# Seven block products in place of eight for the gate and up tiles of a dense feed-forward

## The chip, the cores and the metric
The kernel runs on one core of a Trainium2 chip. Its time is device microseconds (us) of one execution. The engines are TensorE (PE), VectorE (DVE), ScalarE (ACT), GpSimd (POOL) and SyncE (SP), which issues most of the DMAs.

## What is computed
A backbone of two layers over 512 tokens (256 of context, 256 latent) of width 1024. Each layer is a norm, a mixed token stage, a norm and a feed-forward; layer 0 has a dense one, layer 1 experts. The change is in the dense one:

```python
def swiglu(t, w_gu, w_down):
    g, u = jnp.split(t @ w_gu, 2, axis=-1)
    return (jax.nn.silu(g) * u) @ w_down
# layer 0: t is 512 x 1024 float32, w_gu 1024 x 5632, w_down 2816 x 1024
```

## The kernel before
Tokens lie along the free axis: the state is held transposed, as eight 128-row tiles of 512 columns (columns 0 to 255 are context, 256 to 511 latent). Every float32 product is made from three float32r ones: each operand is split in a high part (a rounded copy, made on ACT) and a low part (the operand less its high part, on DVE), and `three` issues high x high, high x low and low x high as three matmuls into one PSUM tile. The state is split once per norm into `hhi` and `hlo`. The weights stream through `raw`, five slots filled by SP's DMAs, and are split unit by unit into `whi` and `wlo`, three slots each (`split_hi` L623, `split_lo` L628), three units ahead of TensorE.

The feed-forward runs in two blocks of 11 column tiles (`FJ`). In a block, each tile j has a gate unit and an up unit of 1024 columns (8 k-tiles of 128x128). `fm_tile` makes each with 8 x 3 matmuls of 512 columns. ACT takes silu of the gate from PSUM into `sg`, DVE multiplies it with the up tile into `hf` (L2155), ACT rounds that into `fhi` (L1573), POOL makes `flo` (L1708). Then eight down units of 1408 columns (11 k-tiles) follow; each gives 33 matmuls of 512 columns and DVE adds the result to `xT` (L2162). Two gate/up tiles share the first walk over k (`two_tiles`), since the state comes tile by tile from the norm.

Order between engines is by semaphores, and each engine runs its own list in order: `split_used` counts units that TensorE is done with, `hi_ready` and `lo_ready` the splits, `sg_ready`, `fh_ready`, `fhi_ready`, `flo_ready` the steps after a pair, `down_out` the down tiles. SP loads a unit when the unit five before it has its low part.

The modulation of layer 1 is made in between: its weights land in `nraw` and `lraw`, TensorE multiplies them at the norms, ACT copies a row to `modrow`, `mod_turns` transposes it on TensorE (L744), and `mods_in` reduces it on DVE. `TURN_AT` says after which unit of the block `mod_turns` is called; the next call waits for `mod_out` of the last. In this kernel:

```python
TURN_AT = {6: NORM1[1] // 2 + 1, 8: NORM1[3] // 2 + 1}
```

## Time and profile before

| | us |
|---|---|
| time, median of 3 runs (1382.73 to 1383.71) | 1383.51 |
| the profiled execution | 1380.24 |
| its span, first to last instruction | 1378.4 |
| first gate/up stretch and second, about 364 to 487 and 549 to 672 | 123 each |
| the down tiles behind each | 62 and 62 |
| mean granted TensorE clock, as a share of full speed | 0.974 |

The page gives busy time and its share of the span for each engine, then the span in 40 slices of 34.5 us in tenths. A timeline row is start, duration, engine, line, operation, output and inputs with their sizes; in brackets the engine's idle time before it and what ended it. "x2" is two instructions in one row, its duration from the first's start to the last's end. Matmuls overlap, so the distance between their starts counts, not their duration.

### The profile page before, as it was taken

To read this page: it belongs to the slowest core of one execution; us is meant where nothing else is said; L and a number is where in the kernel's file an instruction comes from. 1 tells how busy PE (TensorE), PEld (TensorE's weight loads), DVE (VectorE), ACT (ScalarE), POOL (GpSimd) and SP (SyncE) were. 2 spreads that over 40 slices of the span, in tenths; PEclk is the share of its full clock that TensorE was granted. 3 is DMA by queue.
4 is the path that set the end of the run, shared out by engine and by line. 5 is a ranking of instruction groups with operands and counts; after the bars stand their busy time and mean duration, and the time that the engine had idled before them with its cause. 6 is when DMAs were issued, how large, how long until landed. Compare 5 with 4: busy or idle time off the path is not lost.

```text
span 1378.4 us, 19621 instructions
## 1 busy us (share of the span) xinstructions
PE 1284.8 (93%) x7072; PEld 1010.4 (73%) x7072; DVE 812.1 (59%) x1185; ACT 685.9 (50%) x977; POOL 115.8 (8%) x86
## 2 busy tenths in 40 slices
PE   4999977799999999999999987788999999999997
PEld 1688744458688888888886984476888888888876
DVE  2222686753533332332335657666988988988896
ACT  5422342552622221322325543355877877887784
POOL 2200000002011100111120000011000000000070
PEclk9999979899999999999999998899999999999999
DMA  9532246247222322223311354637999999999995
GB/s 357 152 107 92 77 157 242 92 154 271 64 93 94 127 84 77 92 92 117 113 58 53 123 166 179 235 125 284 401 353 375 389 360 363 402 365 359 389 383 208
DMA packets 96847, 283.30 MB, mean 206 GB/s; under 512 B 8704, under 2 KB 10256, under 8 KB 96528
## 3 DMA queue, kind: packets, MB, share of 16 engines
q1 hardware_dynamic: 90880, 264.27, 53.5%
q0 software_dynamic: 3600, 12.58, 2.5%
q10 hardware_dynamic: 2304, 5.58, 1.0%
q8 instruction: 43, 0.70, 0.2%
q14 instruction: 20, 0.16, 0.0%
HBM read 270.86 MB, written 11.53 MB: 205 GB/s over the span
## 4 chain that ended last, share of the span: by engine, by line
PE 81%; DVE 8%; ACT 5%; DMA 3%; issue 2%; SPq 0%; ACTq 0%; DVEq 0%
PE ps L751 13%; PE ps L753 13%; PE ps L752 13%; PE ps L1193 6%; PE ps L1195 6%; PE ps L1194 6%; PE ps L1210 3%; PE ps L1212 3%; PE ps L1208 3%; PE ps L728 2%; DMA raw<-in_w_mod 2%; PE ps L844 2%; PE ps L845 2%; PE ps L846 2%; DVE wlo L628 1%
## 5 line engine op out<-in xcount | busy, mean ns | idle before, releaser
L628 DVE TENSOR_TENSOR wlo<-raw,whi 128x1024 fp32r<-128x1024 f32 (+2 forms) x271 | 350.8, 1310 | 251.3 <-ACT whi L623 249.7
L623 ACT ACTIVATE whi<-raw 128x1024 fp32r<-128x1024 f32 (+2 forms) x271 | 298.1, 1107 | 208.6 <-PE ps L753 138.1
L751 PE MATMUL ps<-hhi,whi 128*128 128x512 f32 (+1 forms) x736 | 275.7, 375 | 7.6 <-DVE hlo L1845 5.9
L752 PE MATMUL ps<-hlo,whi 128*128 128x512 f32 (+1 forms) x736 | 272.8, 371 | 0.0
L753 PE MATMUL ps<-hhi,wlo 128*128 128x512 f32 (+1 forms) x736 | 272.7, 371 | 0.0
L751 PEld LDWEIGHTS ps<-hhi,whi 128*128 128x128 f32 x736 | 138.7, 188 | 41.8 <-issue 10.6
L753 PEld LDWEIGHTS ps<-hhi,wlo 128*128 128x128 f32 x736 | 138.7, 188 | 26.8
L752 PEld LDWEIGHTS ps<-hlo,whi 128*128 128x128 f32 x736 | 138.9, 189 | 25.9
L628 DVE TENSOR_TENSOR xlo<-raw,xhi 128x1024 fp32r<-128x1024 f32 (+1 forms) x98 | 134.4, 1374 | 29.1 <-ACT xhi L623 28.2
L623 ACT ACTIVATE xhi<-raw 128x1024 fp32r<-128x1024 f32 (+1 forms) x98 | 114.3, 1167 | 37.6 <-PE ps L1212 19.6
L1193 PE MATMUL ps<-whi,hs_hi 128*128 128x512 f32 (+1 forms) x256 | 95.4, 373 | 0.9 <-DVE hs_lo L2221 0.9
L1195 PE MATMUL ps<-whi,hs_lo 128*128 128x512 f32 (+1 forms) x256 | 93.2, 364 | 0.0
L1194 PE MATMUL ps<-wlo,hs_hi 128*128 128x512 f32 (+1 forms) x256 | 93.2, 364 | 0.0
L753 PE MATMUL ps<-fhi,wlo 128*128 128x512 f32 x176 | 69.3, 394 | 0.0
L752 PE MATMUL ps<-flo,whi 128*128 128x512 f32 x176 | 69.3, 394 | 0.0
L751 PE MATMUL ps<-fhi,whi 128*128 128x512 f32 x176 | 69.3, 394 | 0.0
L1573 ACT ACTIVATE fhi<-hf 128x512 fp32r<-128x512 f32 x22 | 13.9, 632 | 99.2 <-DVE hf L2155 99.2
L728 PE MATMUL ps<-raw,c_act 128*2 128x512 f32 x272 | 42.8, 706 | 18.1 <-DMA raw<-in_w_mod 17.3
L1700 POOL TENSOR_TENSOR rs<-rs,sq 128x512 f32<-128x512 f32 (+1 forms) x24 | 39.8, 1656 | 223.7 <-ACT sq L1325 223.0
L2162 DVE SCALAR_TENSOR_TENSOR xT<-ps,mod,xT 128x256 f32<-128x256 f32 x32 | 14.0, 479 | 74.1 <-PE ps L753 74.1
L1193 PEld LDWEIGHTS ps<-whi,hs_hi 128*128 128x128 f32 x256 | 48.1, 188 | 9.3 <-issue 1.9
L1195 PEld LDWEIGHTS ps<-whi,hs_lo 128*128 128x128 f32 x256 | 48.1, 188 | 8.2
(336 smaller groups left out, 2056.0 us busy)
## 6 DMA issues: line engine op xcount, KB each, us to landing
raw<-in_w_gu SPq DMA_DIRECT2D x230, 512.0 KB, 5.9
raw<-in_w_dn SPq DMA_DIRECT2D x80, 704.0 KB, 8.4
raw<-in_w_mod SPq DMA_DIRECT2D x68, 512.0 KB, 4.5
raw<-in_w_fm SPq DMA_DIRECT2D x32, 512.0 KB, 3.5
raw<-in_w_out SPq DMA_DIRECT2D x16, 512.0 KB, 4.2
y_rows<-zrow POOLq DMA_DIRECT2D x1, 5120.0 KB, 20.7
mraw<-in_w_mod SPq DMA_DIRECT2D x8, 512.0 KB, 5.9
raw<-in_w_tg SPq DMA_DIRECT2D x8, 512.0 KB, 3.5
```

Source lines behind the costliest of these rows:

```text
L623: nc.scalar.activation(high(v)[:, 0:cols], src[:, 0:cols], ACT.Copy).then_inc(hi_ready, 1)
L628: nc.vector.tensor_tensor(low(v)[:, 0:cols], landed_in(v)[0][:, 0:cols], high(v)[:, 0:cols].bitcast(F32), ALU.subtract).then_inc(lo_ready, 1)
L728: mm = nc.tensor.matmul(ps[32 * kk:32 * kk + 2, PAIR_BANK(n), :], c_act[:, 4 * half + kk, :], units[kk // 2][0][:, kk % 2 * 512:kk % 2 * 5 ...
L751: nc.tensor.matmul(outp, whs, xh, start=first, stop=False)
L752: nc.tensor.matmul(outp, whs, xl, start=False, stop=False)
L753: return nc.tensor.matmul(outp, wls, xh, start=False, stop=last)
L1193: nc.tensor.matmul(o, hs_hi[:, k, :], wh, start=(k == 0), stop=False)
L1194: nc.tensor.matmul(o, hs_hi[:, k, :], wl, start=False, stop=False)
L1195: mm = nc.tensor.matmul(o, hs_lo[:, k, :], wh, start=False, stop=(k == KT - 1))
L1208: nc.tensor.matmul(o, ehi[:, j, :], high(v)[:, w:w + n], start=(j == 0), stop=False, skip_group_check=True)
L1210: nc.tensor.matmul(o, ehi[:, j, :], low(v)[:, w:w + n], start=False, stop=False, skip_group_check=True)
L1212: mm = nc.tensor.matmul(o, elo[:, j, :], high(v)[:, w:w + n], start=False, stop=(j == FJ - 1), skip_group_check=True)
```

## The change
The 512 tokens are halved (context, latent), the eight k-tiles are halved, and gate and up are the two halves of the output: a 2 x 2 x 2 block product. A scheme with seven products of blocks makes it in place of eight. `part_product` makes one product: 4 k-tiles x 3 matmuls of 256 columns. Four of the seven use sums and differences of weight blocks (`weight_sum`, four 128x512 operations on POOL for each pair, into `sq` and `xn`), four use sums of state blocks (made once, on DVE, in `h_sums`, `h_differences` and `t_lo`). Each part of the weights, 512 columns, is split by itself, eight parts ahead (`part_hi_of`, `part_lo_of`), into eight windows of the old `whi` and `wlo`. DVE combines the products from PSUM (`combine`, five operations) into the gate in `sg` and the up tile in `hf`; ACT takes silu of `sg`, DVE multiplies the two (`up_gated`).

The first three pairs of block 0 are made as before, and under them the state's sums: `h_sums` before unit 0's step on DVE, `h_differences` in unit 1's, the low parts in the steps of units 2, 3 and 5. The other 8 pairs of block 0 and all 11 of block 1 are groups of seven. The modulation's last transposes move from units 6 and 8 to 1 and 2, because `mr4` takes the place of `modrow`; the four units in `lraw` are loaded after block 1's gate/up tiles, because `tm` lies there. Many semaphores of two layers become one that counts on; what waits for what stays. The core of the diff (renamed semaphores and their waits are left out):

```diff
--- before.py
+++ after.py
...
-        modrow = sb("modrow", [P, 2, 512])
+        part = ExitStack()
+        modrow = sb("modrow", [P, 2, 512], F32, part)
+        part.close()
+        mr4 = sb("mr4", [P, 4, CTX], F32R)
...
+        fsum = sb("fsum", [P, 2, FJ, T], F32, part)
...
+        tm = sb("tm", [P, 19, CTX], F32R, region)
...
+        def wide(x, a):
+            return fsum[:, x, a:a + 2, :].rearrange("p a (b n) -> p (a b) n", n=CTX)
+
+        x12, x22, t3 = wide(1, 9), wide(1, 7), wide(1, 5)
+        t1, t2, t4 = wide(0, 9), wide(0, 7), wide(0, 5)
...
+        J0, JN, G0 = (3, 0), (FJ - 3, FJ), (0, FJ - 3)
+        PARTS = 7
+        S2, S1, S3, S4 = sq[:, 0, :], sq[:, 1, :], xn[:, 0, :], xn[:, 1, :]
+        S_OF = {1: (S2, 2), 3: (S3, 3), 4: (S1, 1), 6: (S4, 4)}
...
-        TURN_AT = {6: NORM1[1] // 2 + 1, 8: NORM1[3] // 2 + 1}
+        TURN_AT = {1: NORM1[1] // 2 + 1, 2: NORM1[3] // 2 + 1}
...
+        def place7(i, p):
+            return (p + 6 + min(max(p // PARTS - 2, 0), 4 if i else 1)) % 8
...
+        def part_hi_of(act, i, p):
+            n, x = p // PARTS, p % PARTS
+            kind, q = before_part(i, p)
+            if kind == "part":
+                counted(act, part_done, split_used, i, q)
+            else:
+                act.wait_ge(split_used, i * BLOCK + V0 + q + 1)
+            if x in S_OF:
+                act.wait_ge(wsum_ready, 4 * (G0[i] + n) + S_OF[x][1])
+            else:
+                unit_landed(act, i, unit_of(i, n, x == 5))
+            q = place7(i, p)
+            count_one(nc.scalar.activation(whf[:, 512 * q:512 * q + 512], part_source(i, p), ACT.Copy),
+                      part_hi, hi_ready, p)
+
+        def part_lo_of(dve, i, p):
+            counted(dve, part_hi, hi_ready, i, p)
+            q = place7(i, p)
+            count_one(nc.vector.tensor_tensor(wlf[:, 512 * q:512 * q + 512], part_source(i, p),
+                                              whf[:, 512 * q:512 * q + 512].bitcast(F32), ALU.subtract),
+                      part_lo, lo_ready, p)
...
+                sp.wait_ge(split_used, (blocks - 1) * BLOCK + v0 + 2 * FJ)
+                for unit in norm2u:
+                    dst, arrived, _count = mod_landed(unit[1], unit[2])
+                    sp.dma_start(dst, source(unit)[0]).then_inc(arrived, 16)
...
+            def part_product(i, p):
+                n, x = p // PARTS, p % PARTS
+                g = G0[i] + n
+                counted(pe, part_lo, lo_ready, i, p)
+                if g == 0:
+                    if x == 0:
+                        pe.wait_ge(sg_ready[0], J0[0])
+                    if x == 1:
+                        pe.wait_ge(fh_ready[0], J0[0])
+                    if x in (1, 3, 4, 5):
+                        pe.wait_ge(tlo_ready, {1: 1, 3: 2, 4: 5, 5: 4}[x])
+                elif x == 0:
+                    pe.wait_ge(first_out, g)
+                elif x in (1, 3, 4, 6):
+                    pe.wait_ge(comb_out, 5 * (g - 1) + {1: 1, 3: 2, 4: 4, 6: 5}[x])
+                if i and n == 0 and x == 3:
+                    pe.wait_ge(down_out[0], i * KT + 1)
+                xh, xl = [(lambda k: hhi[:, k, 0:CTX], lambda k: hlo[:, k, 0:CTX]),
...
+                bank = (0, 2, 1, 5, 4, 3, 6)[x]
+                for k in range(4):
+                    c = 512 * place7(i, p) + P * k
+                    mm = three(ps[:, bank, 0:CTX], whf[:, c:c + P], wlf[:, c:c + P], xh(k), xl(k),
+                               k == 0, k == 3)
+                count_one(mm, part_done, split_used, p)
...
+                            if r in TURN_AT:
+                                mod_turns(TURN_AT[r])
+                    for p in range(PARTS * JN[i]):
+                        part_product(i, p)
+                    pe.wait_ge(comb_out, 5 * (G0[i] + JN[i] - 1) + 4)
...
+            def gate_silu(l, i, n):
+                act.wait_ge(comb_out, 5 * (G0[i] + n) + 5)
+                j = J0[i] + n
+                nc.scalar.activation(sg[:, j % 2, :], sg[:, j % 2, :], ACT.Silu).then_inc(sg_ready[l], 1)
...
+                        if r == 2:
+                            t_hi(tm[:, 0:4, :], t2, t_ready, 2)
+                            t_hi(tm[:, 8:12, :], t3, hsum_ready, 3)
+                        if r == 3:
+                            act.wait_ge(modT_done, NORM1[3] // 2 + 1)
+                            t_hi(mr4[:, :, :], t4, t_ready, 3)
+                        if r == 2 * J0[i] - 1:
+                            act.wait_ge(split_used, v0 + 2 * J0[i])
+                            t_hi(hhi[:, B12[0], B12[1]], t1, t_ready, 1)
...
+                    for n in range(JN[i]):
+                        g, j = G0[i] + n, J0[i] + n
+                        for x in range(PARTS):
+                            if x == 0:
+                                if i * FJ + j >= 2:
+                                    act.wait_ge(flo_ready[l], i * FJ + (j - 1))
+                                counted(act, part_done, split_used, i, PARTS * n)
+                                nc.scalar.activation(hf[:, j % 2, 0:CTX], ps[:, 0, 0:CTX], ACT.Copy
+                                                     ).then_inc(first_out, 1)
+                            if PARTS * n + x + 8 < PARTS * JN[i]:
+                                part_hi_of(act, i, PARTS * n + x + 8)
+                            if x == 1 and n:
+                                up_hi(l, i, j - 1)
+                            if x == 6:
+                                gate_silu(l, i, n)
+                            for r in range(2 * FJ, 2 * FJ + H):
+                                if behind_part(i, r) == PARTS * n + x:
+                                    unit_landed(act, i, v0 + r)
+                                    counted(act, part_done, split_used, i, PARTS * n + x)
+                                    nc.scalar.activation(high(v0 + r), landed_in(v0 + r)[0], ACT.Copy
+                                                         ).then_inc(hi_ready, 1)
...
+            def weight_sum(i, n, m):
+                g = G0[i] + n
+                a1, a2 = (landed_in(unit_of(i, n, up))[0] for up in range(2))
+                out, in0, in1, op, x = [(S1, a2[:, 0:512], a2[:, 512:1024], ALU.add, 4),
+                                        (S2, S1, a1[:, 0:512], ALU.subtract, 1),
+                                        (S3, a1[:, 0:512], a2[:, 0:512], ALU.subtract, 3),
+                                        (S4, a1[:, 512:1024], S2, ALU.subtract, 6)][m]
+                if m < 2:
+                    unit_landed(pool, i, unit_of(i, n, 1 - m))
+                if g:
+                    counted(pool, part_lo, lo_ready, *((i, PARTS * (n - 1) + x) if n else (0, PARTS * (JN[0] - 1) + x)))
+                if m in (1, 3):
+                    pool.wait_ge(wsum_ready, 4 * g + m // 2 + 1)
+                nc.gpsimd.tensor_tensor(out, in0, in1, op).then_inc(wsum_ready, 1)
...
+                pool.wait_ge(hlo_done, 2 * KT)
+                up_lo(l, 0, 0)
+                for m in range(4):
+                    weight_sum(0, 0, m)
+                for j in range(1, J0[0]):
+                    up_lo(l, 0, j)
...
+                    for n in range(JN[i]):
+                        if n + 1 < JN[i]:
+                            for m in range(4):
+                                weight_sum(i, n + 1, m)
+                        elif i + 1 < blocks:
+                            pass
+                        if n:
+                            up_lo(l, i, J0[i] + n - 1)
+                    up_lo(l, i, FJ - 1)
+                    if i + 1 < blocks:
+                        for m in range(4):
+                            weight_sum(i + 1, 0, m)
...
+            def h_sums():
+                dve.wait_ge(mod_used, NORM1[-1] + 1)
+                dve.wait_ge(hlo_done, 2 * KT)
+                for out, (ks, cs) in ((x12, B12), (x22, B22)):
+                    V.tensor_tensor(out, hhi[:, ks, cs].bitcast(F32), hlo[:, ks, cs].bitcast(F32), ALU.add
+                                    ).then_inc(hsum_ready, 1)
+                dve.wait_ge(hsum_ready, 1)
+                then(V.tensor_tensor(t1, x12, h1, ALU.subtract))
+                V.tensor_tensor(t1, t1, l1, ALU.subtract).then_inc(t_ready, 1)
+
+            def h_differences():
+                dve.wait_ge(t_ready, 1)
+                V.tensor_tensor(t2, x22, t1, ALU.subtract).then_inc(t_ready, 1)
+                dve.wait_ge(hsum_ready, 2)
+                V.tensor_tensor(t3, x22, x12, ALU.subtract).then_inc(hsum_ready, 1)
+                dve.wait_ge(t_ready, 2)
+                then(V.tensor_tensor(t4, h2, t2, ALU.subtract))
+                V.tensor_tensor(t4, t4, l2, ALU.add).then_inc(t_ready, 1)
+
+            def up_gated(l, i, j):
+                dve.wait_ge(sg_ready[l], i * FJ + (j + 1))
+                dve.wait_ge(comb_out, 5 * (G0[i] + j - J0[i]) + 4)
+                V.tensor_tensor(hf[:, j % 2, :], hf[:, j % 2, :], sg[:, j % 2, :], ALU.mult).then_inc(fh_ready[l], 1)
+
...
+            def combine(l, i, n, x):
+                g, j = G0[i] + n, J0[i] + n
+                p1, u3, u2 = hf[:, j % 2, 0:CTX], hf[:, j % 2, CTX:T], sg[:, j % 2, CTX:T]
+                if x >= 2:
+                    counted(dve, part_done, split_used, i, PARTS * n + x)
+                if x == 2:
+                    dve.wait_ge(first_out, g + 1)
+                    V.tensor_tensor(sg[:, j % 2, :].rearrange("p (a n) -> p a n", a=2), ps[:, 1:3, 0:CTX],
+                                    p1.rearrange("p (a n) -> p a n", a=1).broadcast_to([P, 2, CTX]), ALU.add
+                                    ).then_inc(comb_out, 1)
+                if x == 3:
+                    dve.wait_ge(comb_out, 5 * g + 1)
+                    V.tensor_tensor(u3, ps[:, 5, 0:CTX], u2, ALU.add).then_inc(comb_out, 1)
+                if x == 4:
+                    dve.wait_ge(comb_out, 5 * g + 2)
+                    V.tensor_tensor(u2, ps[:, 4, 0:CTX], u2, ALU.add).then_inc(comb_out, 1)
+                if x == 5:
+                    dve.wait_ge(comb_out, 5 * g + 2)
+                    V.tensor_tensor(hf[:, j % 2, :].rearrange("p (a n) -> p a n", a=2), ps[:, 3:5, 0:CTX],
+                                    u3.rearrange("p (a n) -> p a n", a=1).broadcast_to([P, 2, CTX]), ALU.add
+                                    ).then_inc(comb_out, 1)
+                if x == 6:
+                    dve.wait_ge(comb_out, 5 * g + 3)
+                    V.tensor_tensor(u2, ps[:, 6, 0:CTX], u2, ALU.add).then_inc(comb_out, 1)
 
             def ffn(l, v0, blocks):
...
+                    if i == 0:
+                        h_sums()
...
+                        if r == 1:
+                            h_differences()
+                        if r - 1 in TURN_AT:
+                            mods_in(TURN_AT[r - 1])
+                        if r == 2:
+                            t_lo(tm[:, 4:8, :], t2, tm[:, 0:4, :], 1)
+                            t_lo(tm[:, 12:16, :], t3, tm[:, 8:12, :], 2)
+                        if r == 3:
+                            t_lo(tm[:, 16:18, :], t4[:, 0:2, :], mr4[:, 0:2, :], 3)
+                            t_lo(rs2[:, :, :], t4[:, 2:4, :], mr4[:, 2:4, :], 3)
+                        if r == 2 * J0[i] - 1:
+                            t_lo(hlo[:, B12[0], B12[1]], t1, hhi[:, B12[0], B12[1]], 4)
+                        for p in first_parts(r):
+                            part_lo_of(dve, i, p)
+                    if i == 0:
...
+                    for n in range(JN[i]):
+                        for x in range(PARTS):
+                            if x == 0 and n:
+                                up_gated(l, i, J0[i] + n - 1)
+                            combine(l, i, n, x)
+                            if PARTS * n + x + 8 < PARTS * JN[i]:
+                                part_lo_of(dve, i, PARTS * n + x + 8)
...
```

## Rows read from the trace of the kernel before

**Rows 1.** The page's busy time by engine, and POOL's 40 slices.
```profile
PE 1284.8 (93%) x7072; PEld 1010.4 (73%) x7072; DVE 812.1 (59%) x1185; ACT 685.9 (50%) x977; POOL 115.8 (8%) x86
POOL 2200000002011100111120000011000000000070
```

**Rows 2.** Windows over the gate/up stretches: PE, PEld, DVE, ACT, POOL, clock, DMA share, GB/s.
```profile
364.00:487.00 123.00, 123.00 (x531) 98.78 (x530) 41.32 (x44) 40.00 (x52) 14.23 (x11) 1.00 0.31 101
...
549.00:672.00 123.00, 123.00 (x528) 98.58 (x528) 37.84 (x33) 36.66 (x45) 14.19 (x11) 1.00 0.32 103
```

**Rows 3.** Timeline of PE, 512 columns in layer 0, then 256 in layer 1.
```profile
439.86 0.39 PE L751 MATMUL ps<-hhi,whi 128*128 128x512 f32 x1
...
444.06 0.39 PE L751 MATMUL ps<-hhi,whi 128*128 128x512 f32 x1
...
924.82 0.28 PE L751 MATMUL ps<-hhi,whi 128*128 128x256 f32 x1
...
928.90 0.28 PE L751 MATMUL ps<-hhi,whi 128*128 128x256 f32 x1
```

**Rows 4.** Timeline of one gate/up pair: POOL, DVE, ACT, DVE.
```profile
439.40 1.29 POOL L1708 TENSOR_TENSOR flo<-hf,fhi 128x512 fp32r<-128x512 f32 x1 [9.91 <-ACT fhi L1573]
440.30 1.46 DVE L628 TENSOR_TENSOR wlo<-raw,whi 128x1024 fp32r<-128x1024 f32 x1 [1.65 <-ACT whi L623]
443.56 0.60 ACT L1569 ACTIVATE sg<-ps 128x512 f32<-128x512 f32 x1 [3.29 <-PE ps L753]
445.14 1.22 DVE L628 TENSOR_TENSOR wlo<-raw,whi 128x1024 fp32r<-128x1024 f32 x1 [3.37 <-ACT whi L623]
```

**Rows 5.** Timeline at the output projection: DVE, then POOL.
```profile
318.57 1.23 DVE L628 TENSOR_TENSOR wlo<-raw,whi 128x1024 fp32r<-128x1024 f32 x1 [0.28 <-ACT whi L623]
319.14 1.81 POOL L1700 TENSOR_TENSOR rs<-rs,sq 128x512 f32<-128x512 f32 x1 [144.81 <-ACT sq L1325]
```

**Rows 6.** Timeline at the end of layer 1: POOL, then DVE.
```profile
1331.29 2.65 POOL L1737 TENSOR_TENSOR htm<-htm 128x1024 f32<-128x1024 f32 x1
1333.92 4.88 POOL L1734 TENSOR_SCALAR hf<-hf,gate 128x1024 f32<-128x1024 f32 x1
...
1331.60 0.41 DVE L2274 TENSOR_TENSOR eact<-esg,ps 128x256 f32<-128x256 f32 x1
1331.93 0.41 DVE L2229 TENSOR_TENSOR elo<-ps,ehi 128x256 fp32r<-128x256 f32 x1
1332.26 2.77 DVE L628 TENSOR_TENSOR wlo<-raw,whi 128x1024 fp32r<-128x1024 f32 x1
...
1332.26 3.90 DVE L628 TENSOR_TENSOR wlo<-raw,whi 128x1024 fp32r<-128x1024 f32 x2
```

**Rows 7.** Timeline of DVE in the norm, two operations back to back.
```profile
361.13 0.69 DVE L1833 TENSOR_TENSOR xn<-xT,rs 128x512 f32<-128x512 f32 x1
361.74 0.69 DVE L1845 TENSOR_TENSOR hlo<-sq,hhi 128x512 fp32r<-128x512 f32 x1
```

**Rows 8.** Timeline of ACT and DVE: the splits of the first down unit.
```profile
477.65 1.37 ACT L623 ACTIVATE whi<-raw 128x1408 fp32r<-128x1408 f32 x1
...
479.06 1.62 DVE L628 TENSOR_TENSOR wlo<-raw,whi 128x1408 fp32r<-128x1408 f32 x1 [3.21 <-ACT whi L623]
```

**Rows 9.** Timeline at the start of block 0 (DVE, ACT), and at tile 8.
```profile
367.10 0.69 DVE L1845 TENSOR_TENSOR hlo<-sq,hhi 128x512 fp32r<-128x512 f32 x1 [1.01 <-ACT hhi L1339]
...
375.91 0.60 ACT L1569 ACTIVATE sg<-ps 128x512 f32<-128x512 f32 x1 [1.28 <-PE ps L753]
...
407.65 0.18 DVE L1790 TENSOR_REDUCE modsum<-ps 128x8 f32<-128x32 f32 x1
...
409.32 0.60 PE L744 MATMUL ps<-ident,modrow 128*128 128x128 f32 x4
```

**Rows 10.** Windows in layer 0's attention stage (columns as in rows 2).
```profile
238.00:240.00 2.00, 0.00 (x0) 0.00 (x0) 1.93 (x5) 1.54 (x5) 0.00 (x0) 0.67 0.04 8
...
242.00:244.00 2.00, 1.88 (x8) 1.57 (x8) 1.90 (x6) 0.00 (x0) 0.00 (x0) 0.50 0.00 0
244.00:246.00 2.00, 1.86 (x5) 0.51 (x4) 1.93 (x7) 1.88 (x5) 0.00 (x0) 0.62 0.00 0
```

More of the change, by code:

```diff
@@ new lines, in meets, with before_part, behind_part @@
+        def meets(i, p, r):
+            a, b = unit_cols(r)
+            return 512 * place7(i, p) < b and a < 512 * place7(i, p) + 512
+        def before_part(i, p):
+            for q in range(p - 1, -1, -1):
+                if place7(i, q) == place7(i, p):
+                    return "part", q
+            units = (3, 4, 5) if i == 0 else (-3, -2, -1)
+            return "unit", max(r for r in units for q in range(p + 1) if meets(i, q, r))
+        def behind_part(i, r):
+            return max(p for p in range(PARTS * JN[i]) if meets(i, p, r)
+                       and not any(place7(i, q) == place7(i, p) for q in range(p + 1, PARTS * JN[i])))
@@ new lines, in part_lo_of, with first_parts @@
+        def part_lo_of(dve, i, p):
[4 more added lines that the diff above has]
+                      part_lo, lo_ready, p)
+        def first_parts(r):
+            i, r = (0, r) if r < 2 * J0[0] else (1, r - BLOCK)
+            return [p for p in range(8) if before_part(i, p) == ("unit", r)]
@@ L541, in _ @@
             sp.wait_ge(split_used, V_OUT[0] + 1)
-            for unit in norm1u + norm2u:
+            for unit in norm1u:
                 dst, arrived, _count = mod_landed(unit[1], unit[2])
@@ L1562, in ffn @@
                 for i in range(blocks):
-                    for r in range(BLOCK):
+                    for r in range(2 * J0[i]):
                         j = r // 2
-                        if r < 2 * FJ and r % 2 == 0:
-                            act.wait_ge(split_used, i * BLOCK + (v0 + r + 1))
+                        if r % 2 == 0:
+                            act.wait_ge(split_used, v0 + r + 1)
                             if j >= 2:
-                                act.wait_ge(fh_ready[l], i * FJ + (j - 1))
+                                act.wait_ge(fh_ready[l], j - 1)
@@ new lines, in ffn @@
+                    up_hi(l, i, FJ - 1)
+                    if i == blocks - 1:
+                        nc.scalar.preload_act_table_set("natural_log_exp_and_others")
+                    for r in range(2 * FJ, BLOCK):
+                        if r + H < BLOCK or i == blocks - 1:
+                            split_hi(act, v0 + r + H, DUNIT if r + H < BLOCK else UNIT, i)
+                        else:
+                            for p in first_parts(r):
+                                part_hi_of(act, i + 1, p)
+                        if i == blocks - 1:
@@ new lines, in ffn @@
+                    up_gated(l, i, FJ - 1)
+                    for r in range(2 * FJ, BLOCK):
+                        m = r - 2 * FJ
+                        dve.wait_ge(split_used, i * BLOCK + (v0 + r + 1))
+                        for kind, a, b in kinds_of(c0):
+                            g = 2 * (5 * KT + m) + kind
+                            ins = V.scalar_tensor_tensor(xT[:, m, a:b], ps[:, 4 + m % 2, a:b],
+                                                         mod[:, l, g:g + 1], xT[:, m, a:b],
+                                                         ALU.mult, ALU.add)
+                        ins.then_inc(down_out[l], 1)
+                        if r + H < BLOCK or i == blocks - 1:
+                            split_lo(dve, v0 + r + H, DUNIT if r + H < BLOCK else UNIT, i)
+                        else:
+                            for p in first_parts(r):
+                                part_lo_of(dve, i + 1, p)
```

226 lines of the change are left out of this document (137 added, 89 removed).

## The prediction

> **What bounds the kernel now.** I read the page's busy shares first, then the windows over the dense feed-forward, then single instructions in the timelines. Over the whole span TensorE is busy 93% and GpSimd (POOL) 8% [rows 1]. In the dense feed-forward TensorE is busy in all of 123.00 us in each of the two gate/up stretches at full granted clock, VectorE 41.32 and 37.84 us, ScalarE 40.00 and 36.66, GpSimd 14.2, DMA near a third [rows 2]. So TensorE sets this stage and everything else is cover. Inside, 512-column matmuls start every 0.2333 us: 18 of them lie between the two rows at 439.86 and 444.06. The 256-column ones of layer 1 start every 0.1133 us: 36 lie between 924.82 and 928.90 [rows 3]. Half the columns cost half the time; the weight load is hidden at both widths. A gate/up pair is 48 matmuls of 512 columns, 11.2 us.
>
> **What is removed.** A group of seven products is 7 x 4 x 3 = 84 matmuls of 256 columns. At 0.1133 that is 9.52 us, at half of 0.2333 it is 9.80; I take 9.66, or 1.38 us for one product. Against 11.2 us this is 1.54 us a pair and 29.3 us for 19 pairs, if TensorE stays the bound.
>
> **What is added, per group.** DVE: seven lo-splits of 512 columns, one gated product (hf by sg, now both in SBUF), two 512-wide combinations and three 256-wide ones that read PSUM. POOL: four weight sums beside the flo it had, all 128x512 TENSOR_TENSOR. ACT: seven hi-splits, a PSUM copy, silu, fhi. Prices: back-to-back 512-wide DVE operations start 0.61 us apart [rows 7]; 256-wide ones from PSUM 0.33 apart [rows 6]; the one POOL operation of this kind takes 1.29 [rows 4]. DVE alone: 8 x 0.6 + 2 x 0.61 + 3 x 0.33 = 7.0 us. ACT alone: nine of some 0.6 and a copy under that, 5.5 to 6 us. POOL alone: 5 x 1.29 = 6.5 us. Each of the three is under 9.66, and a reading of busy shares would stop here.
>
> **The shared cost.** DVE and POOL do not run side by side. The split at 440.30 takes 1.46 us where the one at 445.14 takes 1.22; it began 0.90 us into flo, which began at 439.40 [rows 4]. So it was held for 0.24 us, and POOL let go at 440.54, some 1.13 us after its start. The other way round, the POOL addition at 319.14 takes 1.81 us because DVE's split (318.57, 1.23 us) was running; 1.29 us before its end is 319.66, so DVE let go 0.14 us before its recorded end [rows 5]. At 1332.26 a DVE split behind a 1024-wide POOL addition takes 2.77 us, while the two DVE operations at 1331.60 and 1331.93, which have one input in PSUM, take their usual 0.41 under the same addition [rows 6]. Each DVE operation with two SBUF inputs therefore excludes each POOL operation of this kind, and the PSUM ones don't. A POOL operation holds 1.13 us; a 512-wide DVE one holds 0.69 - 0.13 = 0.56. A group needs 8 x 0.56 + 5 x 1.13 = 10.1 us of this shared thing. That is above 9.66 and below 11.2: of the 1.54 us a group, 1.1 at most is left.
>
> The Trainium skill (SBUF — State Buffer, Who interferes with whom) states this as an exclusive lock, held for the whole instruction against a DVE instruction with two SBUF inputs. The trace agrees on which operations exclude each other (2.77 against 0.41 us); on how long, its releases come 0.13 to 0.16 us before the recorded ends. What the page's wording would give is a rival below.
>
> **One group stepped.** Take as zero the release of the split after the fourth product. C is a combination (runs freely), L a split, G the gated product, P a POOL operation. C4 0.04; P1 (half sum of up) gets the lock at 0.21; L4 1.34 to 1.90; C5 1.94 to 2.55 beside P2; L5 3.03 to 3.59; C6 beside P3, which ends its hold at 4.72; L6 to 5.28; G, and the next group's L0 and L1, to 7.08, if DVE's next instruction wins against a waiting POOL; P4 beside C2; L2 8.21 to 8.77; C3 beside P5 (flo); L3 9.90 to 10.46. The period is 10.46 us. That DVE wins is taken from one place: POOL's operation of 1333.92 was waiting when the first of two splits from 1332.26 ended, yet the two together take 3.90 us, so the second took its usual time [rows 6]. If POOL wins, P4 comes before G and the period is 10.79.
>
> **Seam and end of a block.** Block 0: after the third old pair ends on TensorE, DVE has G and the residual of t1 (2.4 us) and four splits (to 4.7). S1 of the next group reads a buffer freed by the fifth split, so POOL can do flo, S1 and S2 only from 4.0 to 8.7; with the hi-split, L8 is out at 10.5 and the "third split" at 13.7 us. TensorE asks for that product at 11 x 1.38 = 15.2, so 1.5 us of lead remain, and 0.8 are lost per group. Six periods on, 76.5 us, no weight sums are left. The rest is a chain: C4 to C6 and G (3.9), fhi 0.7, hi of the first down unit 1.37, its lo 1.62 [rows 8], C3 to C5 (8.8, where TensorE may start the first down tile), lo of the second, C6, silu, hi and lo of the third, G, fhi, flo: 17.1 us. The first tile's last k needs that flo and 0.7 us more: 17.9. Block 0 is 76.5 + 17.9 = 94.4 against 8 x 11.2 + 7.7 = 97.3 us now (7.7 is a down tile, 33 matmuls): 2.9 saved. In block 1 the seam is shorter, since the first splits and sums fall under the down tiles: 11.0 + 9 x 10.46 + 17.9 = 123.0 against 11 x 11.2 + 7.7 = 130.9: 7.9 saved. Together 10.8 us.
>
> **The three old pairs.** PE's work is unchanged, but a wait is moved. mod_turns for the last group waits for mod_out, which DVE gives in mods_in; it stood after tile 8 (transposes at 409.32, no idle), now after tile 2 [rows 9]. Tile 2 ends at 375.9 (silu follows at 375.91). DVE ends the norm at 367.7 (367.10 + 0.69, less the overlap), then runs the state's sums first: four 1024-wide (4.8 us at 1.15 each and one drain), lo 3, G, lo 4 (to 375.4), four more sums, lo 5, mods (0.4): 381.8 if undisturbed. POOL's flo gets in between once (1.1 us): 382.7. TensorE idles 6.8 us, with tiles 3 to 5 queued behind it. After a longer idle the granted clock falls: it is 0.67 in 238 to 240 and 0.62 in 244 to 246, after TensorE stood still from 234.6 to 242.1 [rows 10]; so it was low for some 4 us after the restart, and here about 2.3 us are lost. Cost 9.1 us. Bounds: 5.9 and no loss of clock if POOL doesn't intrude; 11.1 + 2.5 if POOL takes every second turn.
>
> **Costed at nothing.** The residuals t_lo (4 us of DVE) and t_hi (ACT) lie under tiles 4 and 5; uncovered they would cost 4. The norm2 loads move behind the second block's down units on SP's queue, ahead of the projection weights; DMA is idle for two thirds there, and they are wanted some 60 us later; uncovered, 2 MB at the stage's 100 GB/s would be 20 us. Merged semaphores issue the same waits.
>
> **Sum.** 10.8 saved, 9.1 lost: -1.7 us. The profiled execution is 1380.24 us (span 1378.4 and 1.84 around it), 3.27 under the median of the runs, so 1378.5 there and 1383.51 - 1.7 = 1381.8 us in the median.
>
> **Rivals.** (1) TensorE stays the bound, since the split work runs eight products ahead and absorbs the lock. For it: 7.0 us of DVE in 9.66. Against: the hold times. 29.3 - 2 x 1.35 for the ends - 9.1 = 17.5 saved: 1366. (2) Slower: POOL takes each contested turn. Periods of 10.79 save 1.1 + 4.9, the early stall is 13.6: +7.6, 1391. It decides where POOL waits while DVE has two excluded operations in a row, above all in the eight 1024-wide state sums. For it: the split at 1332.26 was itself held; against: the pair in 3.90 us. (3) The lock lasts as long as the recorded operations, the wording of the page named above: 8 x 0.69 + 5 x 1.29 = 12.0 us a group, 1.5 more in 15 groups: +21, 1404. Rows 4 to 6 speak against it. (4) The change doesn't do what it says: 256-column matmuls paced by something wider than their columns. Rows 3 exclude it nearly.
>
> **Chances.** Forecast 0.55 (1374 to 1390: per 0.1 us of period 1.5 us, and the stall's bounds), rival 1 0.15, rival 2 0.20, rival 3 0.08, the rest 0.02. 0.2% (2.8 us) is about what a measurement can tell from no change. Of the forecast's 0.55, 0.26 lie below, 0.20 within, 0.09 above; with rival 1 faster, most of 2 and all of 3 slower: faster 0.41, same 0.24, slower 0.35. The range, 1364 to 1396, leaves out rival 3 and the outer parts of 1 and 2. The forecast's own is 1374 to 1390.
>
> **What would show it.** Starts of the first matmul of successive groups: 10.4 to 10.8 us apart in the middle of block 1 if right, 9.7 under rival 1, 12 under rival 3. POOL's sums at 1.7 to 1.8 us mean instead of 1.29, DVE's 512 splits over 1 us mean instead of 0.69. One TensorE gap of 6 to 7 us ended by mod on DVE after tile 2; 11 under rival 2. A gap of some 3 us ahead of each block's first down tile, and one near its end that ends on flo. The forecast is wrong if DVE has idle time waiting for products in the middle of a block.

## The result and the profile after

The changed kernel takes 1393.31 us, median of 6 runs (1388.98 to 1395.96), against 1383.37 us for the kernel before, median of 6 (1382.73 to 1389.97): a ratio of 1.0064, interval [1.0044, 1.0083]. It is slower, by some 10 us; the forecast was 1.7 us faster. The time lies inside the range, and 2 us from the second rival's 1391. The profiled execution has a span of 1390.2 us.

The page's busy times, and POOL's 40 slices (before: [rows 1]):

```profile
PE 1270.5 (91%) x7756; PEld 1033.3 (74%) x7756; DVE 968.2 (70%) x1388; ACT 730.0 (53%) x1095; POOL 242.0 (17%) x162
POOL 2200000002236711667230000011000000000060
```

Windows over the two gate/up stretches, with the columns of [rows 2]: DVE has gone from 41.32 us of 123.00 to 95.42 of 116.50, POOL from 14.2 to 58.61, and TensorE is no longer busy all the time.

```profile
388.00:504.50 116.50, 108.40 (x779) 100.58 (x778) 95.42 (x117) 49.50 (x88) 58.61 (x38) 0.98 0.31 103
552.00:686.00 134.00, 126.89 (x987) 121.09 (x986) 121.71 (x148) 61.59 (x112) 79.59 (x51) 1.00 0.31 110
```

**Where the time came from.** Two operations stand in every kernel of this case: ACT's silu of the first gate tile, for which it waits for TensorE, and DVE's first mixing of a down tile into xT, once in each block. Timeline rows of ACT and DVE, before and then after:

```profile
369.62 0.60 ACT L1569 ACTIVATE sg<-ps 128x512 f32<-128x512 f32 x1 [0.76 <-PE ps L753]
...
490.46 0.87 DVE L2162 SCALAR_TENSOR_TENSOR xT<-ps,mod,xT 128x256 f32<-128x256 f32 x2 [3.42 <-PE ps L753]
...
675.26 0.87 DVE L2162 SCALAR_TENSOR_TENSOR xT<-ps,mod,xT 128x256 f32<-128x256 f32 x2 [3.41 <-PE ps L753]
```

```profile
370.38 0.60 ACT L1732 ACTIVATE sg<-ps 128x512 f32<-128x512 f32 x1 [0.76 <-PE ps L869]
...
505.50 0.88 DVE L2483 SCALAR_TENSOR_TENSOR xT<-ps,mod,xT 128x256 f32<-128x256 f32 x2 [3.08 <-PE ps L869]
...
686.75 0.88 DVE L2483 SCALAR_TENSOR_TENSOR xT<-ps,mod,xT 128x256 f32<-128x256 f32 x2 [3.08 <-PE ps L869]
```

From the first to the second row is block 0: 120.84 us before, 135.12 after, 14.28 more. From the second to the third is block 1: 184.80 before, 181.25 after, 3.55 less. The two together are 10.73 us. What follows the third row differs by 0.3 us (703.14 and 703.45). The 0.76 us by which the first row is late lie ahead of anything that was changed: in the kernels shown here that row falls anywhere from 367.80 to 372.49, so single spans can't be compared to better than some 5 us, and the two block lengths are used below beside the medians.

**The early wait.** TensorE's timeline has one large gap, in front of the transposes of mods:

```profile
387.77 1.09 PE L860 MATMUL ps<-ident,modrow 128*128 128x128 f32 x4 [11.14 <-DVE mod L2024]
```

What DVE and POOL did meanwhile, and the granted clock (the third column from the end) in and behind the gap:

```profile
376.20 2.30 DVE L2394 TENSOR_TENSOR fsum<-fsum 128x1024 f32<-128x1024 f32 x1
378.42 2.29 DVE L2396 TENSOR_TENSOR fsum<-fsum 128x1024 f32<-128x1024 f32 x1
380.63 2.29 DVE L2398 TENSOR_TENSOR fsum<-hhi,fsum 128x1024 f32<-128x1024 f32 x1
382.95 2.17 DVE L2399 TENSOR_TENSOR fsum<-fsum,hlo 128x1024 f32<-128x1024 f32 x1
385.05 2.28 DVE L744 TENSOR_TENSOR wlo<-raw,whi 128x1024 fp32r<-128x1024 f32 x1
...
375.96 1.46 POOL L1918 TENSOR_TENSOR flo<-hf,fhi 128x512 fp32r<-128x512 f32 x1 [26.25 <-ACT fhi L1716]
377.38 2.25 POOL L1914 TENSOR_TENSOR sq<-raw 128x512 f32<-128x512 f32 x1
379.77 2.07 POOL L1914 TENSOR_TENSOR sq<-sq,raw 128x512 f32<-128x512 f32 x1
...
384.00 2.24 POOL L1914 TENSOR_TENSOR xn<-raw,sq 128x512 f32<-128x512 f32 x1
```

```profile
376.00:388.00 12.00, 0.86 (x4) 0.45 (x3) 11.93 (x9) 3.66 (x4) 10.10 (x5) 0.66 0.28 82
387.00:391.00 4.00, 3.23 (x10) 2.77 (x11) 2.86 (x5) 1.06 (x1) 0.00 (x0) 0.50 0.45 135
391.00:395.00 4.00, 4.00 (x13) 3.15 (x13) 0.00 (x0) 0.00 (x0) 0.00 (x0) 0.69 0.00 0
```

Five DVE operations in a row take 2.17 to 2.30 us where a 1024-wide one takes 1.22, and POOL has one operation beside each (the third sum, at 381.80, is among the rows left out). The two engines take strict turns: each of the five DVE operations is held for 0.95 to 1.1 us. The granted clock is 0.50, the lower of its two levels, in 380 to 387.7 and in 388 to 393.4. The 0.69 of 391 to 395 is a mean over its return to full. Behind the gap twelve matmuls of 512 columns start 0.43 us apart, and from 393.66 on they start 0.233 apart: that is 5.9 us after the restart, and the twelve lose some 2.4 us.

**One group.** First matmul of the same product in two successive groups, PE's timeline in block 1. They are 10.92 us apart, and so are the four periods from 601.33 to 645.01 in the mean; in block 0 the four from 441.92 to 485.57 are 10.91. Then one period of DVE and of POOL:

```profile
612.26 0.36 PE L867 MATMUL ps<-tm,whi 128*128 128x256 f32 x1 [0.43 <-DVE sg L2413]
...
623.18 0.36 PE L867 MATMUL ps<-tm,whi 128*128 128x256 f32 x1 [0.43 <-DVE sg L2413]
```

```profile
636.22 1.73 DVE L604 TENSOR_TENSOR wlo<-raw,whi 128x512 fp32r<-128x512 f32 x1
...
639.90 1.44 DVE L604 TENSOR_TENSOR wlo<-raw,whi 128x512 fp32r<-128x512 f32 x1
641.27 1.79 DVE L2404 TENSOR_TENSOR hf<-hf,sg 128x512 f32<-128x512 f32 x1
...
639.05 1.74 POOL L1914 TENSOR_TENSOR xn<-raw 128x512 f32<-128x512 f32 x1
640.76 1.75 POOL L1914 TENSOR_TENSOR xn<-raw,sq 128x512 f32<-128x512 f32 x1
```

POOL's fourth sum starts at 640.76, while the split of 639.90 has the turn. When that split lets go, the gated product (641.27) is ready as well; it takes 1.79 us instead of 0.68, so POOL went first. Grouped by line over 590 to 670, the splits' means are 1.26, 1.17 and 0.68 us with no idle time before them, the gated product's 1.78:

```profile
L604 DVE TENSOR_TENSOR wlo<-raw,whi 128x512 fp32r<-128x512 f32 x22 | 27.6, 1256 | 0.0
...
L2404 DVE TENSOR_TENSOR hf<-hf,sg 128x512 f32<-128x512 f32 x7 | 12.5, 1783 | 0.0
```

**The ends of the blocks.** The same pair of gaps stands in both; here block 1's, on PE's timeline:

```profile
677.67 0.50 PE L867 MATMUL ps<-fhi,whi 128*128 128x512 f32 x1 [2.13 <-DVE hf L2424]
685.75 0.50 PE L867 MATMUL ps<-fhi,whi 128*128 128x512 f32 x1 [0.81 <-POOL flo L1918]
```

### The profile page after: what moved, and what is told of

Its sections match the earlier page's. It is cut to its first block, busy times and chain, and to the rows that moved or that the text cites. A ratio compares the mean times of both kernels' runs of the same rounds, so it can differ in the third digit from the quotient of the medians.

```text
span 1390.2 us, 21735 instructions
## 1 busy us (share of the span) xinstructions
PE 1270.5 (91%) x7756; PEld 1033.3 (74%) x7756; DVE 968.2 (70%) x1388; ACT 730.0 (53%) x1095; POOL 242.0 (17%) x162
## 4 chain that ended last, share of the span: by engine, by line
PE 63%; DVE 18%; issue 10%; ACT 5%; DMA 3%; POOL 1%; SPq 0%; DVEq 0%; ACTq 0%; POOLq 0%
PE ps L867 7%; PE ps L868 7%; PE ps L869 7%; PE ps L1343 6%; PE ps L1344 6%; PE ps L1345 6%; DVE wlo L604 4%; PE ps L1360 3%; PE ps L1362 3%; PE ps L1358 3%; PE ps L844 2%; DMA raw<-in_w_mod 2%; PE ps L960 2%; PE ps L961 1%; PE ps L962 1%
## 5 line engine op out<-in xcount | busy, mean ns | idle before, releaser
L744 DVE TENSOR_TENSOR wlo<-raw,whi 128x1024 fp32r<-128x1024 f32 (+2 forms) x227 | 291.3, 1302 | 138.6 <-ACT whi L739 136.9
L739 ACT ACTIVATE whi<-raw 128x1024 fp32r<-128x1024 f32 (+2 forms) x227 | 250.1, 1110 | 183.8 <-PE ps L869 113.1
L867 PE MATMUL ps<-hhi,whi 128*128 128x256 f32 (+1 forms) x736 | 244.4, 332 | 8.1 <-DVE hlo L2076 4.1
L868 PE MATMUL ps<-hlo,whi 128*128 128x256 f32 (+1 forms) x736 | 240.6, 327 | 0.0
L869 PE MATMUL ps<-hhi,wlo 128*128 128x256 f32 (+1 forms) x736 | 240.3, 327 | 0.0
L604 DVE TENSOR_TENSOR wlo<-raw,whi 128x512 fp32r<-128x512 f32 x57 | 71.5, 1254 | 2.3 <-ACT whi L598 2.3
L1948 POOL DMA_INDIRECT xg<-h_rows,slot_tok x8 | 10.7, 1338 | 329.1 <-DVE slot_tok L2553 328.8
L1721 ACT ACTIVATE sg<-sg 128x512 f32<-128x512 f32 x19 | 12.0, 633 | 84.0 <-DVE sg L2429 84.0
```

The costliest lines, as they stand in the source:

```text
L604: count_one(nc.vector.tensor_tensor(wlf[:, 512 * q:512 * q + 512], part_source(i, p), whf[:, 512 * q:512 * q + 512].bitcast(F32), ALU.subt ...
L739: nc.scalar.activation(high(v)[:, 0:cols], src[:, 0:cols], ACT.Copy).then_inc(hi_ready, 1)
L744: nc.vector.tensor_tensor(low(v)[:, 0:cols], landed_in(v)[0][:, 0:cols], high(v)[:, 0:cols].bitcast(F32), ALU.subtract).then_inc(lo_ready, 1)
L867: nc.tensor.matmul(outp, whs, xh, start=first, stop=False)
L868: nc.tensor.matmul(outp, whs, xl, start=False, stop=False)
L869: return nc.tensor.matmul(outp, wls, xh, start=False, stop=last)
```

## Experiments

The theory at this point: DVE's operations with two SBUF inputs and POOL's reading ones exclude each other, POOL gets its turn after each DVE operation, and both the early gap and the period follow from that. The time by which a POOL operation delays a DVE one is called its hold. Rivals: DVE's work by itself is too long; the sums come too late; the early gap is only the order of mods.

**1. Mods ahead of the state's sums.** The one edit on DVE in block 0:

```diff
                     if i == 0:
+                        mods_in(TURN_AT[1])
                         h_sums()
```

> The changed kernel with one call moved on VectorE: the reduction of the modulation (mods_in) for which TensorE waits after tile 2 stands ahead of the state's sums. Theory (an early wait plus shared-port groups): the one TensorE gap of 11.1 us after tile 2 goes, with the 2 to 2.5 us of low clock behind it; the groups keep their 10.9 us. Time some 13 us under the changed kernel, about 1380 us, ratio to the kernel before 0.996 to 0.999. Rival (the state sums' 10 us of VectorE only move the loss to the seam of the third pair): the gap reappears there, time near 1390. Rival (the groups carry the whole loss): time near 1393.

Measured: 1381.45 us, 10 runs; ratio to before 0.998 [0.9957, 1.0002]. The gap is gone, block 0 is 122.71 us (371.64 to 494.35) instead of 135.12, and the groups stay 10.90 to 10.92 us apart (601.12, 612.04, 622.94, 633.86). So the moved wait cost 12.4 us (11.9 by the medians), and what remains is a kernel level with the one before: without that wait the block products lose 1.9 us in block 0 (122.71 against 120.84) and gain 3.1 us in block 1 (181.74 against 184.80).

**2. The sums without reads.** Each POOL sum becomes two fills of the same tile, which leaves the weight sums out; mods stay where the change has them:

```diff
-                nc.gpsimd.tensor_tensor(out, in0, in1, op).then_inc(wsum_ready, 1)
+                nc.gpsimd.memset(out, 0.0).then_inc(twice, 1)
+                pool.wait_ge(twice, 4 * g + m + 1)
+                nc.gpsimd.memset(out, 0.0).then_inc(wsum_ready, 1)
```

> The changed kernel with each of GpSimd's weight sums replaced by two memsets of the same tile, one waiting for the other: same waits, same signals, about the same length, but nothing is read. The weight sums are left out, so four of seven products are of zeros. Lock theory (only a GpSimd operation that reads excludes VectorE's two-input operations): VectorE's 512-wide splits go back to 0.69 us mean but for those beside flo, the group's period falls from 10.9 to about 9.7 us, and the early gap from 11.1 to 6 to 7 us; time about 1366 to 1371 us. Rival (the period comes from VectorE's own list, from the PSUM banks or from the order of waits, all of which are kept): period stays at 10.8 to 10.9, time above 1388.

Measured: 1376.57 us, one run. The splits are back at 0.69 us, only the one beside flo is held (1.00), and DVE now waits for ACT, that is for buffers that TensorE frees. On DVE's timeline one period, 9.92 us, and on PE's the early gap:

```profile
619.82 0.69 DVE L605 TENSOR_TENSOR wlo<-sq,whi 128x512 fp32r<-128x512 f32 x1 [0.45 <-ACT whi L599]
...
622.32 1.00 DVE L605 TENSOR_TENSOR wlo<-xn,whi 128x512 fp32r<-128x512 f32 x1
...
629.74 0.69 DVE L605 TENSOR_TENSOR wlo<-sq,whi 128x512 fp32r<-128x512 f32 x1 [0.45 <-ACT whi L599]
```

```profile
385.72 1.08 PE L861 MATMUL ps<-ident,modrow 128*128 128x128 f32 x4 [6.98 <-DVE mod L2027]
```

The reads of POOL's sums are the cause of 1 us a group and of 4.2 us of the early gap; the other 7.0 are DVE's own work and one flo. The time is 5.6 us above the 1371 that the theory expected at most; TensorE alone needs 9.92 us a group and not 9.66 (the last section has the rows), which is 4.9 us in 19 groups.

**3. The gated product from PSUM.** With mods first, silu goes to a free PSUM bank and the gated product reads it there:

```diff
-nc.scalar.activation(sg[:, j % 2, :], sg[:, j % 2, :], ACT.Silu)
+nc.scalar.activation(ps[:, 7, :], sg[:, j % 2, :], ACT.Silu)
...
-V.tensor_tensor(hf[:, j % 2, :], hf[:, j % 2, :], sg[:, j % 2, :], ALU.mult)
+V.tensor_tensor(hf[:, j % 2, :], hf[:, j % 2, :], ps[:, 7, :], ALU.mult)
```

> e1 with silu written to PSUM bank 7, so that VectorE's gated product has only one input in SBUF and is no longer excluded. If the period is the sum of the hold times (8 x 0.56 + 5 x 1.13), it falls by 0.56 to about 10.4 us and the time by 8 us against e1, to about 1372. If it is what stepping the order gives (each GpSimd operation holds up the next two-input operation for what no PSUM operation covers), the hold moves from the product to the split behind it, and flo, which comes earlier, loses its cover: period 10.7 to 10.9, time within 3 us of e1.

Measured: 1382.3 us, 10 runs; ratio 0.9993 [0.9969, 1.0017]; groups 10.95 us apart. DVE's timeline:

```profile
628.15 0.68 DVE L2404 TENSOR_TENSOR hf<-hf,ps 128x512 f32<-128x512 f32 x1
628.75 1.20 DVE L604 TENSOR_TENSOR wlo<-sq,whi 128x512 fp32r<-128x512 f32 x1
629.87 1.79 DVE L604 TENSOR_TENSOR wlo<-raw,whi 128x512 fp32r<-128x512 f32 x1
```

The gated product is free of the lock now, 0.68 instead of 1.78, and the two splits behind it pay instead. To take one operation out of the exclusion moved the hold to the next ones and didn't remove it, as the second reading of the expectation said.

**4. Everything on DVE.** Mods first, and the four sums and flo of each group are issued by DVE in its own order; POOL has nothing left here:

```diff
+            def weight_sum(i, n, m):
...
+                V.tensor_tensor(out, in0, in1, op).then_inc(wsum_ready, 1)
...
+                            if x == 2 and n:
+                                up_lo(l, i, J0[i] + n - 1)
+                            if x >= 4 and n + 2 < JN[i]:
+                                weight_sum(i, n + 2, x - 4)
+                            if x == 0 and 2 <= n + 1 < JN[i]:
+                                weight_sum(i, n + 1, 3)
```

> e1 with the weight sums and flo of all groups of seven on VectorE instead of GpSimd (GpSimd keeps only the first sums of each block and the first three flo). VectorE has 13 two-input operations at 0.60 us and 2.2 us of combinations, 10.0 us a group, and nothing that excludes it. Lock theory: period 10.0 to 10.1 instead of 10.9 us though VectorE has five operations more; 15 groups x 0.85 us, with shorter ends some 14 us under e1, about 1366 us, below both kernels. Rival (VectorE's own work is what the groups wait for): five more operations lengthen the period to 13 us, time above 1400.

Measured: 1362.94 us, 4 runs; ratio 0.9862 [0.9834, 0.989]. DVE runs back to back without being held once, five operations more per group, and a group takes 10.02 us (two rows of its timeline below). TensorE is busy all through 560 to 640. The period is what the lock theory expected, the time 3 us below its 1366. This is 18.5 us faster than the first experiment, with the same arithmetic, and faster than both kernels.

```profile
611.74 0.68 DVE L604 TENSOR_TENSOR wlo<-sq,whi 128x512 fp32r<-128x512 f32 x1
...
621.75 0.68 DVE L604 TENSOR_TENSOR wlo<-sq,whi 128x512 fp32r<-128x512 f32 x1
```

**5. The sums on DVE, flo on POOL.** As the fourth experiment, but flo (`up_lo`) stays on POOL.

> The four weight sums of each group are put on VectorE, the residual flo stays on GpSimd; mods still come ahead of the state's sums. With everything on VectorE a group was 15 operations 0.605 us apart and three 0.33 apart, 10.02 us. Theory of holds and turns: flo leaves VectorE (-0.605) and its hold on GpSimd (1.07 to 1.13) takes the place, less what falls beside an operation that reads PSUM: 10.0 to 10.5 us a group, 1363 to 1371 us. Rival (the sums cost what they cost because GpSimd delivers them late, not by exclusion): VectorE would be at 9.4 us and TensorE at 9.92 the bound, under 1362 us.

Measured: 1361.28 us, 4 runs; ratio 0.9835 [0.9782, 0.9888]. The fourth and the fifth are not told apart by their intervals. Block 0 is 113.85 us and block 1 172.26, 7.0 and 12.5 less than before. The period is 9.92, TensorE's own, and the time is under 1362: both are what the expectation's rival forecast, by which the sums cost time because POOL delivers them late, and the theory allowed 10.0 at the least. But the theory missed by the size of one hold. Flo holds DVE for 0.50 and not for 1.07, so DVE needs 10.02 - 0.605 + 0.50 = 9.92 us as well (it is busy 78.29 of 80.00 us), and this run doesn't tell the two accounts apart. Against late sums speak the changed kernel, where DVE has no idle time before its splits and they themselves take longer, and the third and sixth experiment. DVE, then POOL:

```profile
621.42 0.68 DVE L604 TENSOR_TENSOR wlo<-raw,whi 128x512 fp32r<-128x512 f32 x1
622.02 0.68 DVE L2422 TENSOR_TENSOR sg<-ps,hf 128x512 f32<-128x512 f32 x1
622.62 1.18 DVE L604 TENSOR_TENSOR wlo<-xn,whi 128x512 fp32r<-128x512 f32 x1
...
621.06 2.19 POOL L1918 TENSOR_TENSOR flo<-hf,fhi 128x512 fp32r<-128x512 f32 x1 [7.73 <-ACT fhi L1716]
```

Here flo, begun 0.36 us before the split of 621.42, let that split pass: it took 2.19 us, 0.90 more than its 1.29, and DVE lost only 0.50, since half the hold fell beside the combination that reads PSUM. So POOL does not win each contested turn. What decides one is open: in the changed kernel's early gap flo (375.96) began 0.24 us before the DVE sum of 376.20 and went ahead of it. The Trainium skill (SBUF — State Buffer, Who interferes with whom) gives the turn to whichever issues first. By the recorded starts the alternation of the early gap agrees with that, and the split of 621.42 does not.

**6. One sum made twice.** Mods first; POOL makes the fourth sum of each group a second time:

```diff
+                if m == 3:
+                    nc.gpsimd.tensor_tensor(out, in0, in1, op).then_inc(twice, 1)
+                    pool.wait_ge(twice, g + 1)
                 nc.gpsimd.tensor_tensor(out, in0, in1, op).then_inc(wsum_ready, 1)
```

> As the kernel with mods first, and the fourth weight sum of each group is made twice on GpSimd: one more 512-wide addition of two SBUF inputs per group, its result the same. Theory of holds and turns: some 1.0 us more per group where it meets VectorE's back-to-back splits, half of that where it falls beside operations that read PSUM: period 11.4 to 12.0 instead of 10.91, 15 groups, 1389 to 1398 us. Rival (GpSimd has slack, 36 of 50 us busy, and VectorE is held by its own order): 10.91 us and 1381 to 1382.

Measured: 1407.6 us, 4 runs; ratio 1.0161 [1.0112, 1.0211]; groups 12.60 to 12.63 us apart (607.10, 619.73, 632.33, 644.96). The direction is the theory's, the size is beyond it: one operation of 1.29 us costs 1.7 us a group, some 25 us in all. With a sixth reading operation next to the four sums and flo, three DVE operations in a row are held, where the change has only the first of them held (DVE's timeline):

```profile
613.81 1.78 DVE L2408 TENSOR_TENSOR hf<-hf,sg 128x512 f32<-128x512 f32 x1
615.51 1.79 DVE L605 TENSOR_TENSOR wlo<-sq,whi 128x512 fp32r<-128x512 f32 x1
617.22 1.75 DVE L605 TENSOR_TENSOR wlo<-raw,whi 128x512 fp32r<-128x512 f32 x1
```

The rows account for the 1.7 us. The sum made again (POOL, 615.12) holds the split of 615.51 for 1.11 us. Flo, which now comes right behind it (616.71), holds the split of 617.22 for 1.07; in the first experiment flo (632.65) held one split for 0.49 (1.17 instead of 0.68), since the rest of it fell beside a combination. 1.11 + 1.07 - 0.49 = 1.69 us a group. DVE has no idle time in these rows, so the 2.83 us in which POOL then stands still, until a split frees the buffer of the next first sum, add nothing: the second addition costs 1.11 itself, and the rest because it pushes flo out of its cover.

**7. Sums of one input.** From the changed kernel, to ask why the prediction's row for a contested turn misled:

```diff
-                nc.gpsimd.tensor_tensor(out, in0, in1, op).then_inc(wsum_ready, 1)
+                nc.gpsimd.tensor_scalar(out, in0, 1.0, None, ALU.mult).then_inc(wsum_ready, 1)
```

> As the changed kernel, but each of GpSimd's four weight sums is a multiplication of one input by 1.0 (TENSOR_SCALAR, the kind of the row from which the prediction took that VectorE wins a contested turn); the second input is left out, so the block products are wrong. If the kind decides who wins: TensorE's early gap is 7 us instead of 11.1 and the period 10.4 to 10.5, about 1382. If GpSimd wins with this kind as well: gap 11, period 10.9, about 1390 to 1393. If this kind isn't excluded at all: gap 7, period 9.92, about 1376.

Measured: 1377.97 us, one run; early gap 8.27 us; block 1 172.03 us, the same as in the second experiment. None of the three cases fits wholly; the third, "not excluded at all", comes nearest, and TensorE doesn't wait in the groups of block 1. The kind matters, but by its hold: this kind still gets turns and holds DVE for far less. DVE's state sums in the early gap take 1.62, 1.21 and 1.51 us instead of 2.29, so 0 to 0.4 us each:

```profile
377.07 1.62 DVE L2396 TENSOR_TENSOR fsum<-fsum 128x1024 f32<-128x1024 f32 x1
378.62 1.21 DVE L2398 TENSOR_TENSOR fsum<-hhi,fsum 128x1024 f32<-128x1024 f32 x1
379.87 1.51 DVE L2399 TENSOR_TENSOR fsum<-fsum,hlo 128x1024 f32<-128x1024 f32 x1
```

The operation from which the prediction read that DVE wins was a TENSOR_SCALAR [rows 6], this kind, and not a TENSOR_TENSOR. The trace of before also has a third split right behind those two, next to the same POOL operation:

```profile
1336.09 2.45 DVE L628 TENSOR_TENSOR wlo<-raw,whi 128x1408 fp32r<-128x1408 f32 x1
```

A split of this width takes 1.62 us by itself [rows 8], so this one was held for some 0.8. The pair in 3.90 us was not the whole of what that place shows.

**8. Sums in halves.** From the changed kernel, each sum as two of 256 columns:

```diff
-                nc.gpsimd.tensor_tensor(out, in0, in1, op).then_inc(wsum_ready, 1)
+                nc.gpsimd.tensor_tensor(out[:, 0:256], in0[:, 0:256], in1[:, 0:256], op).then_inc(twice, 1)
+                pool.wait_ge(twice, 4 * g + m + 1)
+                nc.gpsimd.tensor_tensor(out[:, 256:512], in0[:, 256:512], in1[:, 256:512], op).then_inc(wsum_ready, 1)
```

> As the changed kernel, but each weight sum on GpSimd is made as two of 256 columns, one waiting for the other. If what counts is the sum of GpSimd's holds: the early gap stays at 11 us and the period at 10.9 (some more for two starts), 1390 to 1396. If what counts is the number of VectorE operations that meet one whole GpSimd operation: the gap falls to some 9 us and the period towards 10.4, about 1384.

Measured: 1389.0 us, one run; early gap 9.27 us; groups 10.75 us apart (604.42, 615.17, 625.92, 636.65). In the early gap each DVE operation meets one POOL operation and is held for that one alone: the state sums take 1.63 to 1.75 us, held for 0.4 to 0.5. Here, where DVE has few operations and POOL much work, the number of turns counts, as the second reading said (9 us). In the groups nearly the whole of POOL's time is needed anyway, DVE idles 1.35 us a group behind ACT, and the period moves by 0.16 only. Neither reading holds in both places.

## Why the prediction was wrong

It read the right mechanism, that the two engines exclude each other, and went wrong mainly at one step: "if DVE's next instruction wins against a waiting POOL". Where it decides most, POOL took its turn after each DVE operation.

- **TensorE no longer the bound, rival 1 out.** Right. 9.92 us of matmuls run in 10.91 us groups, DVE has no idle time before its splits, and rival 1's world exists only where the two-input sums are gone from POOL (second, fifth and seventh experiment).
- **Which operations exclude each other.** Right. Combinations with a PSUM input keep 0.68 and 0.41 us, splits and the gated product go up to 1.79; beside fills on POOL splits keep 0.69. A POOL turn costs DVE 1.07 to 1.11 us (1.79 - 0.68), against 1.13 in the sum. The longer lock of rival 3 (12.0 us a group) is out: 10.91.
- **The period.** 10.46 forecast, 10.91 measured. The fourth sum comes ahead of the gated product (rows of 640.76 and 641.27), as in rival 2's 10.79; by the prediction's own stepping that order is 0.33 of the 0.45. The other 0.12 is not resolved. Over the 15 periods of the sum this is 6.8 us; the nine in block 1 make 4.1 of the 4.4 us between 7.9 saved and 3.55.
- **The early wait.** 6.8 + 2.3 = 9.1 us forecast. The place, the queue behind it and the price of the low clock (2.3 forecast, some 2.4 in the twelve matmuls) were right. POOL got in five times and not once: the gap is 11.14 us, rival 2's 11.1, and the first experiment prices the whole at 12.4. The forecast counted one operation of POOL there, though five were ready: the same step, at the place where it is dearest.
- **TensorE's own time.** 9.66 us a group was taken, 9.92 measured. It mattered only where TensorE is the bound. Rival 1 without its early loss of 9.1 would be 1357; the fifth experiment is that case and takes 1361.3, and 19 groups by 0.26 are 4.9 us, which covers the difference.
- **Block 0 apart from the wait.** 2.9 us saved forecast, 1.9 lost in the first experiment (122.71 against 120.84), so 4.8 apart. Six periods of 0.45 more are 2.7 of it. At the seam TensorE waits 0.80 and 1.43 us there, where the forecast left it a lead of 1.5; why DVE's splits come later than stepped was not followed further.
- **Ends.** A gap of some 3 us and one that ends on flo were forecast; 2.13 and 0.81 measured.
- **POOL's sums at 1.7 to 1.8 us.** Two of the four are (1.75 each); one has 1.52, and the first 1.29, since it starts as DVE runs a combination.

The sum by measured terms: 12.4 (wait) + 1.9 (block 0) - 3.1 to - 3.55 (block 1) = 10.7 to 11.2 us, against 10.73 in the two profiled executions and a difference of the medians of 9.94. Between the forecast's -1.7 and 10.73 lie 12.4 us: 3.3 in the wait, 5.0 in the periods by the turn, 1.8 by the unresolved 0.12, and 2.3 at the seams and ends.

The rival with the right numbers had 0.20. The evidence against it was one pair of splits beside a POOL operation of another kind, with a held split right behind it, and the prediction named the eight state sums as the place where this decides. A row of the same operation on both sides was not in the trace of before; the two prices should then have stood as the two ends, with no preference from that row.

## What to carry to other kernels

Two engines whose own work is 7.0 and 6.5 us can together set the period of a group that TensorE does in 9.92, and then work can be cheaper on one of them alone: a 512-wide sum costs DVE 0.605 us when it makes it itself and up to 1.11 us when POOL makes it beside. Put POOL's reading operations where DVE has operations that read PSUM, or take them off POOL altogether. When a wait is moved ahead, list everything that its producer has queued before it, and price that queue at its contested durations and not at its free ones.

## What the runs showed of the hardware

Against a DVE operation with two SBUF inputs, a fill on POOL holds nothing (splits keep 0.69 us), a one-input 512-wide operation 0 to 0.4 us, a two-input 512-wide one 1.0 to 1.11 (0.5 where the rest falls beside a DVE operation that reads PSUM), and a 256-wide one 0.4 to 0.5.

Turns alternate where DVE runs 1024-wide sums back to back, but a lone flo lost its first turn to a 512-wide split (2.19 us). Which of two waiting engines goes first isn't known beforehand from these runs.

Matmuls of 256 columns have two paces at the same granted clock of 1.00. In the kernel with everything on DVE, 18 matmuls of the same kind take 2.04 us early in block 0 and 2.12 in a later group. Over whole stretches the distance between starts is 0.1133 us in the first four products of the changed kernel and over 930 to 940 in layer 1, and 0.118 in its later groups; in the first and fifth experiment it is 0.118 from the second product on. 512 columns stay at 0.2333:

```profile
396.17 0.28 PE L867 MATMUL ps<-tm,whi 128*128 128x256 f32 x1
...
398.21 0.28 PE L867 MATMUL ps<-tm,whi 128*128 128x256 f32 x1
...
610.08 0.28 PE L867 MATMUL ps<-hhi,whi 128*128 128x256 f32 x1
...
612.20 0.28 PE L867 MATMUL ps<-hhi,whi 128*128 128x256 f32 x1
```

84 at 0.118 are the 9.92 us of the second and fifth experiment. The cause of the two paces was not tested. The slower one is a floor under the kernels shown here, 0.4 us a group above what the faster pace would give.
